# Attention scores in a bidirectional encoder: second pass of the split product with 64 rows per softmax instead of 128

## The reference

```python
# 8 heads, HEAD_DIM 64, V_DIM 128, 1024 keys
s = jnp.einsum('bqhcd,bkhcd->bhcqk', q_blk, k, preferred_element_type=jnp.float32)
p = jax.nn.softmax(s, axis=-1)
a = p[:, :, 0] - lam * p[:, :, 1]
return jnp.einsum('bqhk,bkhe->bqhe', a.astype(v.dtype), v)
```

## Time and profile before

| | |
|---|---|
| median of 3 runs | 2625.18 us (2624.01 to 2626.92) |
| span of the profiled execution | 2624.8 us |
| instructions in it | 30478 |
| mean granted clock of TensorE | 0.987 |
| TensorE products of the scores, L483 and L484 | 256 each, medians 0.39 to 0.50 us long |
| minima of VectorE, L950 | 128, 154.9 us busy, 12.2 us idle before them |

### The profile page before, as it was taken

One profiled execution on the slowest core, in us unless ns is written; L12 is line 12 of the kernel. 1 busy time (PEld: TensorE's weight loads), 2 busy tenths in 40 slices (PEclk: granted clock), 3 DMA queues, 4 the chain that ended last, 5 costly groups with the idle time before them and its releaser, 6 DMA issues.

```text
span 2624.8 us, 30478 instructions
## 1 busy us (share of the span) xinstructions
PE 2517.0 (96%) x11476; PEld 2059.2 (78%) x11476; DVE 1437.6 (55%) x1148; ACT 842.2 (32%) x1036; POOL 750.0 (29%) x573
## 2 busy tenths in 40 slices
PE   7999789989999999999999899999999999999996
PEld 5788677777778888888888778888888888888884
DVE  7545699999345444444444544444444444444446
ACT  4111388878332222222222321112322222222222
POOL 2122255655342222222222342223322222222220
PEclk9999899999999999999999999999999999999998
DMA  3332321121111111111111111111111111111111
GB/s 119 129 112 96 96 65 51 54 55 57 72 41 49 48 48 48 48 48 48 48 48 48 40 41 50 50 51 42 48 49 48 48 48 48 48 48 48 48 48 64
DMA packets 41933, 150.53 MB, mean 57 GB/s; under 512 B 5024, under 2 KB 5408, under 8 KB 41888
## 3 DMA queue, kind: packets, MB, share of 16 engines
q1 hardware_dynamic: 41888, 149.92, 16.7%
HBM read 133.12 MB, written 16.78 MB: 57 GB/s over the span
## 4 chain that ended last, share of the span: by engine, by line
PE 74%; issue 6%; POOL 5%; DVE 2%; ACT 1%; POOLq 0%; DVEq 0%; ACTq 0%
PE PS L224 72%; POOL Yl L1136 1%; POOL cu L1129 1%; POOL XGh L1094 1%; PE PS L483 1%; POOL Yl L1094 1%; POOL sq L1142 1%; PE PS L506 0%; DVE XGl L274 0%; PE PS L484 0%; PE PS L491 0%; POOL coef L1123 0%; POOL coef L1120 0%; PE PS L245 0%; DVE X L1082 0%
## 5 line engine op out<-in xcount | busy, mean ns | idle before, releaser
L218 POOL TENSOR_TENSOR Wl<-Wraw,Wh 128x1024 fp32r<-128x1024 f32 x196 | 474.6, 2422 | 1618.0 <-ACT Wh L213 1618.0
L224 PE MATMUL PS<-XGh,Wh 128*128 128x512 f32 x2176 | 674.9, 391 | 27.9 <-POOL Wl L218 23.8
L224 PE MATMUL PS<-XGl,Wh 128*128 128x512 f32 x2176 | 672.0, 390 | 0.0
L224 PE MATMUL PS<-XGh,Wl 128*128 128x512 f32 x2176 | 671.8, 390 | 0.0
L213 ACT ACTIVATE Wh<-Wraw 128x1024 fp32r<-128x1024 f32 x196 | 208.0, 1061 | 1174.5 <-PE PS L224 1076.7
L224 PEld LDWEIGHTS PS<-XGh,Wh 128*128 128x128 f32 x2176 | 409.3, 189 | 115.6 <-issue 22.7
L224 PEld LDWEIGHTS PS<-XGl,Wh 128*128 128x128 f32 x2176 | 409.7, 188 | 85.8
L224 PEld LDWEIGHTS PS<-XGh,Wl 128*128 128x128 f32 x2176 | 409.5, 188 | 85.7
L1033 DVE TENSOR_TENSOR X<-PS,X 128x1024 f32<-128x1024 f32 x160 | 193.9, 1222 | 159.0 <-PE PS L224 158.7
L224 PE MATMUL PS<-Hh,Wh 128*128 128x512 f32 x704 | 224.3, 400 | 8.5 <-issue 8.5
L224 PE MATMUL PS<-Hh,Wl 128*128 128x512 f32 x704 | 223.8, 399 | 0.0
(11 more groups left out here) (142 smaller groups left out, 2809.5 us busy)
## 6 DMA issues: line engine op xcount, KB each, us to landing
Wraw<-weights SPq DMA_DIRECT2D x196, 512.0 KB, 3.2
X<-k_scratch SPq DMA_DIRECT2D x28, 256.0 KB, 3.8
X<-q_scratch SPq DMA_DIRECT2D x28, 256.0 KB, 3.8
X<-x_tiles SPq DMA_DIRECT2D x8, 512.0 KB, 9.2
q_scratch<-X SPq DMA_DIRECT2D x8, 512.0 KB, 2.6
v_scratch<-X SPq DMA_DIRECT2D x8, 512.0 KB, 2.6
k_scratch<-X SPq DMA_DIRECT2D x8, 512.0 KB, 3.0
acc<-v_scratch SPq DMA_DIRECT2D x8, 512.0 KB, 3.2
```

The source lines that it names most:

```text
L218: pool.tensor_tensor(Wl[:, s, :], Wraw[:, s, :], Wh[:, s, :].bitcast(F32), ALU.subtract).then_inc(w_lo, 1)
L224: ins = pe.matmul(ps[:, h * HALF:(h + 1) * HALF], w, m[:, h * HALF:(h + 1) * HALF], start=begin, stop=last and w is wl)
```

## The change

The first pass (query high and low times key high, 128 rows) stays. The second pass is taken out of the first one's loop and set behind both slots' first products, as products of 64 rows: rows 0 to 63 for c = 0, rows 64 to 127 for c = 1, with the two softmaxes taking turns. For c = 1 the query's low part is now written to rows 0 to 63, so that the high part stands in rows 64 to 127. The second pass thus gives q high times k low; the product q low times k low is no longer computed, and in the first pass both parts are there as before. `s_done` is raised after each slot's last product of the second key half.

```diff
                         cols = slice(half * HALF, (half + 1) * HALF)
                         qs = Q_of(h)[c][:, q * P:(q + 1) * P]
                         pe.matmul(slot(c)[:, cols], qs, Kh[parity][c][:, cols], start=True, stop=False)
-                        ins = pe.matmul(slot(c)[:, cols], qs, Kl[parity][c][:, cols], start=False, stop=True)
-                    ins.then_inc(s_done, 1)
+                for half in range(2):
+                    for c in range(2):
+                        rows, cols = slice(c * HD, (c + 1) * HD), slice(half * HALF, (half + 1) * HALF)
+                        ins = pe.matmul(slot(c)[:, cols], Q_of(h)[c][rows, q * P:(q + 1) * P], Kl[parity][c][rows, cols],
+                                        start=False, stop=True)
+                        if half == 1:
+                            ins.then_inc(s_done, 1)
...
             def q_lo(h, c, part, src):
 
-                up, cols = slice(HD, P), slice(part * HALF, (part + 1) * HALF)
+                low, cols = (slice(HD, P), slice(0, HD))[c], slice(part * HALF, (part + 1) * HALF)
                 dve.wait_ge(qh_made, 4 * h + 2 * part + c + 1)
-                dst = Q_of(h)[c][up, cols]
-                dve.scalar_tensor_tensor(out=dst, in0=src[c][up, cols], scalar=-SCALE, in1=dst.bitcast(F32),
+                dst = Q_of(h)[c][low, cols]
+                dve.scalar_tensor_tensor(out=dst, in0=src[c][low, cols], scalar=-SCALE, in1=dst.bitcast(F32),
                                          op0=ALU.mult, op1=ALU.subtract).then_inc(ql_made, 1)
```

## The result

| | before | after |
|---|---|---|
| median of 4 runs | 2625.4 us | 2646.23 us (2644.37 to 2648.42) |
| ratio | | 1.0077, 95% interval 1.0063 to 1.0091 |
| span of the profiled execution | 2624.8 us | 2642.5 us |

The change makes the kernel 20.8 us slower by the medians (the interval of the ratio is 17 to 24 us); 2636.5 had been forecast, in a range of 2627 to 2655.

A forecast was written before the change was run, and what follows sets the result against it. VectorE was taken as the fuller engine in attention, with the TensorE-ScalarE loop close behind. Heads 1 to 6 (8.1), head 0 (1.3) and head 7 (1.3 and 0.6) sum to 11.3 us on 2625.2: 2636.5, range 2627 to 2655.

The forecast's parts named there:

- rival A: Attention stage: half-height products run side by side, slower through slot 0's lateness, 2632 to 2644 us; chance 0.62.
- rival B: Attention stage: half-height products take turns, the TensorE-ScalarE loop becomes 6.01 us, the kernel +26, 2651 us; chance 0.19.
- VectorE is the fuller engine, TensorE's saving is worth nothing: Attention stage: VectorE busy 43.8 of a head's 46 us, TensorE 41.0; TensorE's 15 to 30 us saving gains no time.
- Slot 0 complete at E + 1.36: Each step: slot 0's scores finish 1.36 us after E, the end of the second exponential's accumulator read.
- the gap at the change: Between full- and half-height products on TensorE: 0.08 us per change, the middle of 0 and 0.17, two changes a step.
- The late partner: In the half-height pass: a product starting later than its pair adds 0 to 0.10 us once, taken as 0.05.
- The loop grows from 5.39 to 5.60: Loop of TensorE and ScalarE (slot 1's products, transposes, copy, both exponentials): 5.60 us instead of 5.39.
- A head +1.35: Heads 1 to 6: each ends 1.35 us later (bounds +1.0 and +2.2), 8.1 us over the six.
- Head 0 +1.3: First head: no slack of this kind, some six steps at the TensorE-ScalarE loop's pace, 6 x 0.21 = 1.3 us.
- Head 7 +1.9: Last head: 1.3 us up to step 4, then 0.6 from three loop-paced steps.
- Rival C: Not slower: slot 0 ends early enough for VectorE to find it done, gain at half clock, 2622 us; chance 0.12.
- Rival D: Granted clock down at every head start because TensorE has less work, 2641 us; chance 0.07.

The follow-up runs named there:

- hold runs: Kernel before with slot 0's last product moved behind the wait for the second exponential, ahead of slot 1's first (2638.28 us) or last product (2643.25 us).
- own_slot: The change with each slot's products done by itself, so no pairs and four changes of height a step; 2647.5 us, ratio 1.0080 to the kernel before.
- low_first: The change with slot 1's low products, paired with slot 0's, ahead of slot 1's high ones; 2637.95 us, ratio 1.0033 to the kernel before.
- unpaired: The change with the half-height pass listed slot by slot (slot 0, slot 0, slot 1, slot 1); 2643.83 us, ratio 1.0065 to the kernel before.

## Why the prediction was right, and where its sizes were off

The direction and the mechanism were right, the size was short in every term. With +20.8 us the time lies outside rival A's own 2632 to 2644 and above the upper bound of its sum, 19; that it lies inside the stated range is luck, for it was rival B that held the range open to 2655, and B's mechanism isn't there.

- **VectorE is the fuller engine, TensorE's saving is worth nothing.** Right in what it led to, but there was next to no saving. One undisturbed head, before and after:

```profile
533.10:578.43 45.33, 40.42 (x249) 33.33 (x248) 43.21 (x46) 37.86 (x68) 26.50 (x45) 0.99 0.21 58
```

```profile
543.24:590.40 47.16, 40.22 (x249) 29.01 (x250) 42.66 (x44) 37.84 (x68) 26.93 (x45) 1.00 0.20 56
```

TensorE is busy 0.2 us less a head, not some 15 to 30 us less in the stage. And after the change VectorE no longer sets the pace: its wait for scores is 47.3 us, where 20 to 30 had been named.

- **Slot 0 complete at E + 1.36.** Right in kind, measured 1.49. The missing 0.13: the second pair comes 0.34 after the first, not 0.23 (0.11), and the gap at the change is 0.10, not 0.08. The 0.08 was the middle of 0 and 0.17, my estimate from a product's listed length beyond its pitch; that a change costs what this length says, no run shows. What I had no term for is the second 0.10 of every change. The late partner (0.05) doesn't exist: pairs start within 0.02 us.
- **The loop grows from 5.39 to 5.60.** It grows to 5.73: the transposes start at E + 1.38 instead of + 1.30, and ScalarE's copy 1.13 after them instead of 1.08 (423.05 to 424.18), behind the second change of height. I had treated the loop as a side condition: the hold and own_slot runs show that its growth carries at least as much of an undisturbed head's loss as slot 0's lateness. In the hold runs 0.22 us of loop cost 0.86 a head, 0.69 us of lateness another 0.6.
- **A head +1.35.** Measured +1.84, so 11.6 instead of 8.1 for heads 1 to 6; the upper bound had been 2.2 a head. Up to the minimum of step 3 the working holds almost to the digit: named 17.82 us after the head's first minimum, measured 17.81 (399.56 to 417.37), against 16.30 before. The step that failed is the one behind it, where slack at steps 3 to 7 was to take some of this back: those steps lost another 0.3 us instead, three of them at the loop's 5.73 to 5.78 us.
- **Head 0 +1.3.** This is the term that failed: +5.6. "Head 0 has no slack of this kind; some six steps run at the TensorE-ScalarE loop's pace" left out steps 0 and 1, where the pipeline fills and the second exponential alone decides. The loss is 1.4, 2.1, 1.4 and 0.8 us in steps 0 to 3 of the change and nothing in sum behind them. Some 2.7 us of it are the lateness of steps 0 and 1 (the estimate above); part of the rest is the clock, 0.76 over head 0 instead of 0.85. How much of it, and whether the lateness itself lets the clock fall, stays open.
- **Head 7 +1.9.** Measured +3.4, of which some 0.6 is the granted clock at its start, 0.76 instead of 1.00.
- **Rival B (no side by side)** named 2651 and a time near the measured one, for a reason that isn't there: pairs run. **Rival C** needed slot 0 within E + 0.45 at step 1; it came at 1.49. **Rival D** named 2641, with the granted clock down at every head start; that less work on TensorE would bring this was my guess, and no run shows it. In the change it is down at two of the seven starts of heads 1 to 7 (heads 3 and 7, 0.53 and 0.76), as before (heads 4 and 6, 0.76 at both). In low_first it is 0.76 at six of seven, though TensorE's list there is as long as the change's; what decides it, no run shows.

## What to carry to other kernels

Before an engine's work is cut, find the loops that run through it and ask what the cut does to their order: here two slots that had been independent were tied to the later of two exponentials, and the loop went from 5.39 to 5.84 us by the order alone. Half height then gave back 0.11 of it. Half-height pairs must come in runs long enough to pay for what a change of height takes, here some 0.20 us (own_slot): of the 0.46 us that two pairs save, 0.11 were left. And look at the steps where a pipeline fills: there a delay that is otherwise hidden is paid in full (here minima 0.64 and 0.74 us later, steps 0.63 and 0.72 longer).

## What the runs showed of the hardware that I had not expected

- Products in different row halves ran side by side even where another product of the first half stands between them in the list (unpaired: starts 0.01 and 0.02 us apart).
- Across a change between 128 and 64 rows no weights were loaded ahead: the weight loads started with the product (422.38 in the change, 298.44 in unpaired, 432.05 in own_slot), where between neighbours of one height they started 0.23 us ahead of it (298.55 for 298.78). The product after that one is 0.10 us late all the same.
- VectorE's 64x512 split takes 0.69 us alone and 1.65 and 1.99 with most of it beside GpSimd's 128x1024 split (1.21 where only the second half is); moving GpSimd's two splits to other steps is worth 10.9 us of 2626.7 in this kernel.
- Products that nobody reads made the kernel 5.7 us faster (4.3 of it in head 0), with the granted clock at 1.00 instead of 0.85 from 297 to 343 us.
